# The second key step of each pair in four parts between the Newton steps of a chunked recurrence

## The reference, cut to what matters

```python
def fox_block(q, k, v, c_q, c_k, q_pos, k_pos):
    s = jnp.einsum('bqhd,bkhd->bhqk', q, k, preferred_element_type=jnp.float32) * ATTN_SCALE
    s = s + jnp.swapaxes(c_q, 1, 2)[:, :, :, None] - jnp.swapaxes(c_k, 1, 2)[:, :, None, :]
    s = jnp.where(k_pos[None, :] <= q_pos[:, None], s, -jnp.inf)
    p = jax.nn.softmax(s, axis=-1)
    return jnp.einsum('bhqk,bkhd->bqhd', p.astype(v.dtype), v)
```

```python
def rwkv7_step(s, inp):
    r_t, w_t, k_t, v_t, kk_t, a_t = inp
    s_kk = jnp.einsum('bhvk,bhk->bhv', s, kk_t)
    s = s * w_t[:, :, None, :] - s_kk[..., None] * (kk_t * a_t)[:, :, None, :] + v_t[..., None] * k_t[:, :, None, :]
    o = jnp.einsum('bhvk,bhk->bhv', s, r_t)
    return s, o
```

## Time and profile before

| | |
|---|---|
| median of three executions | 1602.19 us |
| the profiled execution | 1604.0 us, span of its instructions 1602.2 us |
| TensorE (matmul) busy | 1538.6 us, 96% of the span |
| VectorE, ScalarE, GpSimd busy | 958.4, 636.5 and 82.1 us |
| the recurrence, 1047.7 to 1280.4 us | 232.7 us, TensorE busy 211.6 |
| DMA | 341.72 MB, mean 213 GB/s |

### The profile page before, as it was taken

The page is one execution under the profiler, slowest core; times in us unless marked ns, Lnnn a source line. Parts: engine busy times, 40 slices in busy tenths (PEclk is TensorE's granted clock), DMA queues, the critical chain, the costliest instruction groups (busy, mean ns, idle before and its releaser), DMA issues.

```text
span 1602.2 us, 35979 instructions
## 1 busy us (share of the span) xinstructions
PE 1538.6 (96%) x14428; PEld 1142.3 (71%) x14428; DVE 958.4 (60%) x2300; ACT 636.5 (40%) x1307; POOL 82.1 (5%) x99
## 2 busy tenths in 40 slices
PE   6999999999999999999989999989898999999998
PEld 5787788888888888888656666678777854444443
DVE  5688846786367666587786656445454458333333
ACT  3246443554345531355655655623323371100011
POOL 1010000000000000000000000000000004222220
PEclk9999999999999999999999999999999999999999
DMA  6366483447534564355897566577656289999893
GB/s 231 124 212 202 173 276 134 163 151 257 169 134 151 196 216 132 106 165 179 282 302 219 177 201 183 170 232 230 191 175 210 92 314 335 358 350 354 326 335 123
DMA packets 184512, 341.72 MB, mean 213 GB/s; under 512 B 22229, under 2 KB 124117, under 8 KB 173654
## 3 DMA queue, kind: packets, MB, share of 16 engines
q1 hardware_dynamic: 166826, 256.32, 49.1%
q0 software_dynamic: 10496, 72.98, 12.2%
q10 hardware_dynamic: 7024, 10.12, 1.7%
HBM read 286.13 MB, written 55.35 MB: 213 GB/s over the span
## 4 chain that ended last, share of the span: by engine, by line
PE 83%; DVE 5%; ACT 5%; DMA 3%; issue 2%; SPq 1%; ACTq 0%; DVEq 0%
PE psum L1073 32%; PE psum L1360 25%; PE psum L1060 7%; PE psum L1046 5%; PE psum L1320 4%; PE psum L1235 3%; PE psum L1306 3%; PE psum L1665 2%; ACT big L1750 1%; PE psum L1119 1%; ACT L1750 1%; DVE big L2368 1%; PE psum L1568 1%; SPq L845 1%; DMA out_shiftP<-big 1%
## 5 line engine op out<-in xcount | busy, mean ns | idle before, releaser
L1073 PE MATMUL psum<-big 128*128 128x256 f32 (+1 forms) x1920 | 433.3, 383 | 0.6 <-ACT zst L1763 0.6
L1073 PEld LDWEIGHTS psum<-big 128*128 128x128 f32 x1920 | 364.4, 190 | 57.7 <-issue 2.0
L1360 PE MATMUL psum<-big 64*64 64x64 f32 (+4 forms) x5440 | 258.9, 272 | 16.2 <-issue 10.1
L1763 ACT ACTIVATE zst<-psum 128x256 f32<-128x256 f32 (+1 forms) x336 | 126.9, 385 | 351.4 <-PE psum L1073 342.9
L1360 PEld LDWEIGHTS psum<-big 64*64 64x64 f32 (+2 forms) x5440 | 179.7, 133 | 101.1 <-issue 74.8
L1073 PE MATMUL psum<-big,wbuf 128*128 128x256 f32 (+1 forms) x768 | 182.9, 386 | 1.9 <-ACT zst L1763 1.8
L1073 PEld LDWEIGHTS psum<-big,wbuf 128*128 128x128 f32 x768 | 146.0, 191 | 27.4 <-issue 5.2
L2368 DVE SCALAR_TENSOR_TENSOR big<-big,pars 128x512 f32<-128x512 f32 x240 | 161.0, 745 | 0.4
L1007 POOL DMA_INDIRECT big<-in_cache_v,pidx x64 | 68.2, 1065 | 639.7 <-PE psum L1320 426.0
L1046 PE MATMUL psum<-ident,big 128*128 128x128 f32 (+2 forms) x558 | 79.5, 281 | 8.7 <-ACT big L2035 3.3
L1750 ACT ACT_TABLE_LOAD x61 | 78.3, 1283 | 13.5 <-DMA big<-in_x_first 7.7
(11 more groups left out here) (333 smaller groups left out, 2027.7 us busy)
## 6 DMA issues: line engine op xcount, KB each, us to landing
big<-in_k_pages SPq DMA_DIRECT2D x432, 128.0 KB, 2.3
big<-wS SPq DMA_DIRECT2D x36, 768.0 KB, 5.8
zst<-in_k_pages SPq DMA_DIRECT2D x80, 128.0 KB, 2.8
wS<-big SPq DMA_DIRECT2D x12, 768.0 KB, 5.8
wbuf<-in_w_pairs SPq DMA_DIRECT2D x18, 512.0 KB, 3.9
big<-in_w_pairs SPq DMA_DIRECT2D x18, 512.0 KB, 4.5
zT<-big ACTq DMA_DIRECT2D x16, 512.0 KB, 3.3
rwS<-big SPq DMA_DIRECT2D x32, 256.0 KB, 4.3
```

The lines of the kernel that those rows point to most:

```text
L1073: last = nc.tensor.matmul(psum[:, bank, 0:wide(p) // 2], left(k), right(k), start=first and k == 0, stop=k == 3, skip_group_check=True)
L1360: return nc.tensor.matmul(out, l, r, start=start, stop=stop, skip_group_check=True)
L1763: nc.scalar.activation(parts_[:, U % 2, COPIED_TO[j], 0:n], psum[:, (0, 1, 2, 0, 1, 2, 3)[j], 0:n], ACT.Copy, scale=0.125 if i == U_QA els ...
```

## The change

The second key step of a pair (`keys(1)`) is taken out from between `increments` and `local`. Its 16 products are cut into four parts of 4 (`keys_part`), and a part stands behind each of the Newton steps l = 2, 3, 4 and 5. The first part carries the two waits that the step had (pages there, PSUM bank read), the last one its signal. VectorE's `key_scores` for it moves ahead of the queries' part. `keys` now does only the first step. SyncE's and ScalarE's programs are as they were.

```diff
-                def keys(j):
-                    n = (2 * i + u) * KPAIR + j
+                def keys_part(part):
+                    n = (2 * i + u) * KPAIR + 1
+                    if part == 0:
+                        pe.wait_ge(k_in[n % NRING], 256 * (n // NRING + 1))
+                        pe.wait_ge(sc_read, KEARLY + n)
+                    e, pr = part // 2, part % 2
+                    for ct in range(4):
+                        last = mm(psum[32 * ct:32 * ct + 32, 7, 0:256].rearrange("p (i c) -> p i c", i=2), qbd[:, pr, (2 * ct + e) * 32:(2 * ct + e + 1) * 32],
+                                  k_ring[n % NRING][:, 2 * ct + e, :, pr, :], part == 0, part == 3)
+                    if part == 3:
+                        last.then_inc(sc_mm, 1)
+
+                def keys():
+                    n = (2 * i + u) * KPAIR
                     if n == 0:
                         pe.wait_ge(o_read, len(ITEMS))
...
-                keys(0)
+                keys()
...
                     inverse(0, l)
                     inverse(1, l)
+                    keys_part(l - 2)
                 solve(0)
                 solve(1)
                 queries(0)
                 queries(1)
                 increments()
-                keys(1)
                 local(0)
                 local(1)
...
                 for l in range(2, 6):
                     for s in range(2):
                         factors(s, l)
+                key_scores(KEARLY + (2 * i + u) * KPAIR + 1, 7)
                 at('st', 8, back=True)
...
                 increments()
-                key_scores(KEARLY + (2 * i + u) * KPAIR + 1, 7)
```

## The result

The change makes the kernel slower by 0.28%: median 1604.69 us of 20 runs against 1600.95 us of 20 runs of the kernel before on the same chip, ratio 1.0028 with a 95% interval of 1.0019 to 1.0038. That is +4.5 us (3.0 to 6.1), where +5.7 was forecast. As a time, 1604.69 us lies inside the forecast's wide range and 0.3 us under its own range of 1605 to 1611: the kernel before has a median of 1600.95 us in these 20 runs, 1.2 us less than in the three that the forecast started from. Single runs were far longer, one of the 20 of the changed kernel (3002 us), one of e3's (3136) and one of e2's (1644), and no ratio rests on them.

What follows compares the result with a forecast made beforehand. TensorE, busy 96% of the span, was taken as the bound; +6.5 blocks, +0.2 waits, +0.5 idles, -1.5 clock made +5.7 us: 1609.7 profiled, median 1607.9 us (+0.36%). Own range 1605 to 1611, wide range 1599 to 1613.

Steps and rivals of the forecast that it cites:

- Starts and stops of the block: On TensorE, each key block loses 0.27 us to switching product form; three more blocks in 8 pairs add 6.5 us.
- Waits of the first part, and `key_scores`: Pages and PSUM bank are ready before the first part, and VectorE idles where key_scores moves: 0 us each.
- Behind the old step: Without the key step, local and the next pair's first products just fit behind VectorE's results: 0.2 us.
- The "issue" idles: TensorE idles with no engine behind them, read as late program blocks: -3.5 us in Newton steps, +4.0 in dense stretches.
- (a): In the Newton steps, earlier pair_load and longer-lasting program blocks take 0.5 us off each of seven idles: -3.5 us.
- The clock: Shorter idles spare half the cost of two falls of TensorE's granted clock to 0.50: -1.5 us.
- The end of the stage: GpSimd's first gathers start about 5 us earlier and TensorE's short bursts move with them: 0 us, -2 to +3.
- The signs I had named: Wrong if a part costs under 0.55 us, idles sum under 8 or over 20, or TensorE waits on pages.
- The rival "nothing measurable": Whole kernel within +0.2% to -0.2%, around 1602 us, with switches at their lower end or (a) larger; chance 0.27.
- The rival "faster": (a) in full: moving pair_load ends the Newton idles and both clock falls; 1594 us, or 1598 with two thirds; chance 0.15.

Runs made afterwards that it cites:

- e3: Kernel before, with page loads of the last 13 key steps cut to 8 of 128 partitions: 1594.03 us, ratio 0.9940 to the kernel before.
- e2: Changed kernel, with the four key parts as two blocks of 8 products behind Newton steps 3 and 5: 1603.63 us, ratio 1.0015 to the kernel before.
- e9: Kernel before, with its second key step cut into four parts laced into the old place: 1605.87 us, ratio 1.0031 to the kernel before.
- e11: Changed kernel, with VectorE's key_scores back behind increments: 1606.10 us, ratio 1.0028 to the kernel before.
- e6: Changed kernel, with SyncE's loads behind the second key step held to about their old time in all pairs: 1613.72 us, ratio 1.0091 to the kernel before.
- e10: Changed kernel, with SyncE's loads held to about their old time only in pairs where pages follow: 1606.35 us, ratio 1.0034 to the kernel before.
- e1: Changed kernel, with all four key parts together behind the fifth Newton step: 1605.31 us, ratio 1.0015 to the kernel before.
- e5: Kernel before, with pair_load sent ahead of the second key step's pages in SyncE's queue: 1600.78 us, ratio 1.0015 to the kernel before.
- e8: Kernel before, with the second key step whole between the two query products and pair_load sent ahead of the pages: 1597.57 us, ratio 0.9995.
- e12: e8 with the first key step also moved over TensorE's wait for the transposes' copy: 1599.87 us, ratio 0.9992 to the kernel before.
- e7: Kernel before, with the second key step whole between the two query products, its key_scores between VectorE's two query parts: 1601.32 us, ratio 1.0020.
- e4: Changed kernel, with key page loads behind the first three steps cut to 8 of 128 partitions: 1598.43 us, ratio 0.9976 to the kernel before.

## Why the prediction was right

The direction, the main term (the blocks) and nearly the size are as forecast: +4.5 us (3.0 to 6.1) against +5.7. That the sum came so near is in part luck, since the term of the idles is not known to better than its own size.

- **Starts and stops of the block.** Forecast 0.27 us a block and 6.5 us; measured 0.30 and 7.2, inside the bounds. The 0.05 us that I had allowed behind a block is real, at 0.04. e9 shows the term by itself: four blocks in the old place give a slowdown of the same size, and its interval of 1.0009 to 1.0052 leaves no room for a free switch. The Trainium skill ("TensorEngine Tiling", section "Key Properties") says that a change of tiling mode drains the engine. The 0.12 us going in and 0.04 behind agree with it in kind.
- **Waits of the first part, and `key_scores`.** 0 and 0: no wait for pages appears in the waits of TensorE, and e11 finds no price of VectorE's move that is clear of the noise.
- **Behind the old step.** I had 0.2 us for tight waits. No wait on line 2800 stands in the list.
- **The "issue" idles.** The mis-sized term. I had -3.5 in the Newton steps and +4.0 in the dense stretches, net +0.5; the profiles have 10.8 to 2.3 = -8.5 and 3.1 to 7.6 = +4.5, with the last idles -4.1 over the stage. Both signs and both places are right, and so nearly is the second size; the first was too small by 5. That these idles are program blocks that come late, which I had only read from a packet count, is borne out by their place at every 256th record and by the q8 packet ahead of each. Of the two reasons that I gave for (a), neither is settled. For the earlier signal: held back, the Newton idles are 4.2 (e6) and 6.8 us (e10) and not 2.3, but these two executions differ from each other by as much, and the medians show about 1 us. For the longer block: in the third pair the 256 records behind 1123.38 took 3.74 us before, and the same stretch of program takes 4.69 us with its parts after (1121.47 to 1126.16), while the q8 packets of a pair start no closer than 3.2 us to each other in any run. That fits, but it was not run by itself, since e2 and e1 change the count of blocks with it.
- **The clock.** Forecast half of the two falls gone, -1.5: one fall went, -1.4.
- **The end of the stage.** Forecast 0: the bursts of the earlier trace rows inside the stage (idles of 1.2 us) went, one idle of 1.1 us and the late copy of 1.2 us came.
- **The signs I had named.** A part costs 0.69 us (0.57 and the 0.12 ahead of it) and not under 0.55; the idles sum to 10.9, between 8 and 20; SyncE's `pair_load` comes at 1111.90 and 1140.41 where it had been near 1116 and 1146. All held. The sum was also nearer than its terms: on the profiled executions the idles gave 4.6 us more than forecast (-4.1 against +0.5), and the medians do not show them. With the execution of before 3 us above its median, and 4.4 us between two executions of one program, most of the -4.1 may be chance.

The rival "nothing measurable" is touched only by the lower edge of the interval, +0.19%. The rival "faster" rested on `pair_load` being what stops the program's arrival in the Newton steps. e5 moved that transfer out and gained nothing. e3 shows what most of the page traffic is worth: 0.6%, with two thirds of the idles left.

What stays open: why a block of program comes late, that is, how its delay divides between pages, `pair_load` and a latency of its own. Open too is where saved time went. By the rest column e1, e8 and e12 save 2.5, 5.5 and 6.4 us against before. In e1 the idles rose by 1.7 us; in e8 and e12 they did not rise (13.4 and 14.6 against 15.0), and these two executions are short, but their times are not told apart from before. A profile of an execution at the median would be needed to tell.

## What to carry to other kernels

Each further block of products of another tiling costs time: here 0.28 to 0.30 us amid two kinds of neighbours, and four blocks in place of one made the kernel slower (e9). So a block cut up to fill gaps can pay only where the timeline shows a gap at that very place. Putting the four together again at the new place was not shown to gain (e1). Before counting on a gain in dense small products, see whether the idles of the engine have another engine behind them. Where they have none, number the engine's records: here all stood 256 records or a multiple of it apart, within two, so they were the program itself coming late, and edits shifted them more than they removed them. And before pricing such idles from profiles of one execution each, look for two executions of the same program: here they differed by 4.4 us.

## What the runs showed of the hardware

TensorE's program comes to it in blocks of 256 records, and a late block is an idle with no engine behind it, up to 2.3 us at a time before, and 3.6 in e12: all 155 such idles of the 14 executions stand at the same place of every 256 records, and each ends 1.2 to 1.6 us after a 16 KB packet of q8 has landed. q8 moves the same 115 packets in every variant, and their own time in the pairs is 1.11 us on average with few pages and 1.12 with all, though the idles were 4.3 us less with few.

The first gathers of GpSimd come with delays of other engines. Where the gathers start behind the last key step (before, e3, e5, e7, e8, e12), TensorE's first idle of 0.36 to 0.39 us ends 1.28 to 1.33 us after the first gather's start, and bursts of six records follow. Where they start behind the last Newton step (the changed kernel, e1, e2, e4, e6, e10, e11), one idle of 1.07 to 1.10 us ends 5.64 to 5.75 us after it; and in the changed kernel a copy of ScalarE starts 1.2 us late. That the gathers cause this is argued from this fixed distance; no run leaves them out.
